# A hybrid decoder step on one core: the second token of each cached compression pair moves to ScalarE's queue, and GpSimd makes one page's product of the sample rows' stick-breaking scores

## The chip, the core and the metric

The kernel runs on one core of one Trainium2 chip, as one program. The metric is the device time of one execution, in microseconds (us). Each time is a median of several executions. The engines are TensorE (PE; its weight loads are PEld), VectorE (DVE), ScalarE (ACT), GpSimd (POOL) and SyncE (SP), which only issues transfers and handles registers. A name with a q (SPq, ACTq) is an engine's instruction queue. Every engine runs its own queue in order, and semaphores order the engines against each other.

## The reference, cut to what matters

The program is one inference step of a one-layer decoder, for a prompt of 512 tokens and for 8 sample rows (one new token each, with 256 cached tokens in two pages of 128). Both go through an input projection, two groups of attention heads, an output projection and a hierarchical mixture of experts. Two pieces of it matter here.

The compression branch folds the cached keys and values, 16 tokens at a time, into blocks (block 32, stride 16):

```python
def compress_blocks(k, pe, w1, w2):
    chunks = k[:, :(nc + ratio - 1) * CMP_STRIDE].reshape(B, nc + ratio - 1, CMP_STRIDE, NSA_KV_HEADS, HEAD_DIM)
    blocks = jnp.concatenate([chunks[:, r:r + nc] for r in range(ratio)], axis=2)
    ...
    hid = jax.nn.gelu(jnp.einsum('bnge,eh->bngh', flat, w1))
    return jnp.einsum('bngh,hd->bngd', hid, w2)
```

The stick-breaking heads of a sample row need, for each of 8 heads, the scores of its query against 256 cached keys of 64 elements:

```python
z = jnp.einsum('bqhd,blhd->bhql', q, k).astype(jnp.float32) / math.sqrt(HEAD_DIM)
```

## The kernel before, in words

**The plan.** Before any instruction is written, the kernel builds one list, `PLAN`, of steps (`step(kind, key)`). Every engine walks this list and emits its own part of each step, so the list is the order of work of all five queues. `Signals` turns the marks made on the way into semaphore values. `side` and `put(slot, ...)` hang further steps on the slots of the projection: slot 2n + half is half `half` of projection tile n. There are 30 tiles, six groups of weight columns (in the order KV4, KV2, SBQ, NQ, SBK, SBV) times five row tiles (four of the prompt with 128 rows, one of the 8 sample rows).

**A projection tile.** TensorE multiplies in two halves of four products (line 2825; 2829 for the 8 rows) into a ring of four PSUM banks. ScalarE copies the result out (2722, 2725). For the groups with rotary positions, GpSimd makes the sine products (2649) and, for some groups, copies (2651 to 2654), counted on the semaphore `swapped`; VectorE makes the cosine product (2785), waits for `swapped` and adds (2787). Two tiles later the tile's results are stored by ScalarE's queue (2592 to 2595) and turned by TensorE (2807). All transposes (`tstep`) go through a ring of two PSUM banks, whose copies alternate between ScalarE (2682) and VectorE (2766, 2768). A transpose waits for the copy of the one two before it.

**The compression pairs.** `pair_step(q)` stands in slots 4 to 25. It turns pair q, 128 rows of two tokens each (`XT`, line 2807 on TensorE), and then plans `load_pair(q + 6)`, as there are PAIRS = 6 buffers. There are 20 pairs: 16 of the cache (eight sample rows, keys and then values) and 4 of the prompt. In `sync_more`, kind "pair" (lines 1033 to 1053), SyncE waits until TensorE has turned pair q - 6 and issues the loads. A cached pair takes four, two pages by two tokens, as every token of a pair lands in its own half of the buffer; a prompt pair takes two (1047). The page numbers come from the input `page_table`: `load_small` (984 to 991) loads it and reads its 16 numbers into registers of SyncE. The same queue carries the compression weights (996) and the next projection weights (2617), interleaved slot by slot. Pairs 0 to 5 are planned ahead of the projection.

**The sample rows' scores.** `query_rows(b)`, for b from 0 to 7, stands in slots 35 to 39, between the last tiles of the group NQ. Its order against the rotation of those tiles is: rotation of NQ tile 2, rounds 0 to 3, rotation of NQ tile 3, rounds 4 to 6, rotation of NQ tile 4, round 7. The query row of b has been stored to memory and is loaded by SyncE spread over all 128 partitions (1064) into one of two buffers; row b + 2 is loaded once round b has been scored (`sb_scored`). Page loads for later steps (1081, 1085, 1088) follow in the same queue. On VectorE a round is, for each of the two pages, a product of 128 x 512 elements (1329) and a sum over the 64 elements of a head (1334).

```python
            for pg in range(NPG):
                n = lq["sbk", 2 * b + pg]
                sg.wait(dve, f"slot{n % SLOTS}", n)
                ins = V.tensor_tensor(product_sb[:, pg, :]...
            link(ins)
```

**What comes behind.** The cached pages of the other branches, the prompt's attention, the output projection, the router and then 16 experts, whose weights (three of 2 MB each) SyncE loads into a ring of eight buffers, each as soon as TensorE is done with it.

Of the kernel before, what the change touches and what calls it, by code (L numbers as in the profile page):

```python
# [15 lines left out]
ALU = mybir.AluOpType  # L16
# [7 lines left out]
P = 128  # L24
D = 1024
SEQ = 512
NB = 8
# [140 lines left out]
def body(nc, ctx, a, out, cf_at, cf_n, cb_at, cb_n):  # L168
# [157 lines left out]
    def query_rows(b):  # L326
        step("qb", b)
        sg.mark("sb_scored", b)
        load_query(b + 2)
        for pg in range(NPG):  # L330
            load_page(lq["sbk", 2 * b + pg] + SLOTS)
# [161 lines left out]
    for n, (cc, i) in enumerate(proj):  # L493
        use("m", ("proj", n), "act")
        norm(n + 2)
        for half in range(2):
            step("proj", n, half)
            if n == 0 and not half:
                transpose_h(1)
            if half:  # L500
                transpose_h(n + 2)
            if half and i == TILES - 1 and n // TILES + 2 < NCH:
                for piece in range(4):
                    put(2 * n + 1 + piece, load_w_more, n // TILES + 2, piece)
            if half and cc >= NQ:
                step("rope", n)
                sg.mark("swapped", n)
# [512 lines left out]
    def pool_page(name, j):  # L1020
        return a[name][0, bass.ds(page_reg[j], 1)].rearrange("o t h d -> (o t) (h d)")

    def sync_more(sp, kind, key):
        if kind == "load_small":
# [7 lines left out]
        elif kind == "pair":  # L1032
            q, = key
            kv, t = order[q]
            if q >= PAIRS:
                sg.wait(sp, "t_full", ("XT", q - PAIRS))
            dst = pair[:, q % PAIRS, :].rearrange("p (g l d) -> p l g d", g=GROUPS, l=2)
            name = "cmp_" + "kv"[kv]
            if t < 2:
                if (kv, t) == (0, 0):  # L1040
                    for i in range(QT):
                        n = pn[KV4, i]
                        sg.wait(sp, f"st_raw{rq[n] % 4}", n)
                        sg.wait(sp, f"st_rot{ri[n] % 2}", n)
                src = out[name + "_p"][0, 0, t * 2 * P:(t + 1) * 2 * P].rearrange("(p l) g d -> p l g d", l=2)
                for l in range(2):
                    sp.dma_start(dst[:, l], src[:, l]).then_inc(sg[f"pair{q % PAIRS}"], 16)
            else:
                for pg in range(NPG):
                    src = a["cache_" + name][0, bass.ds(page_reg[2 * (t - 2) + pg], 1)].rearrange(  # L1050
                        "o (p l) g d -> (o p) l g d", l=2)
                    for l in range(2):
                        sp.dma_start(dst[64 * pg:64 * pg + 64, l], src[:, l]).then_inc(sg[f"pair{q % PAIRS}"], 16)
        elif kind == "q_store":
# [65 lines left out]
    def gps_begin(pool):  # L1120
        nc.gpsimd.iota(token[:, :], [[P, TILES]], base=0, channel_multiplier=1,
                       allow_small_or_imprecise_dtypes=True).then_inc(sg["iota"], 1)

    def gps_more(pool, kind, key):
        if kind == "slots":
            i, = key
# [12 lines left out]
    def act_more(act, link, inverse_rms, kind, key):  # L1139
        if kind == "hid":  # L1140
            kv, = key
# [12 lines left out]
        elif kind == "gates":  # L1154

            sg.wait(act, "swapped", pn[KV2, QT])
            nc.scalar.activation(gates[:, 0:QT, :], gates[:, 0:QT, :], ACT.Exp, scale=-1.0)
# [141 lines left out]
    def dve_more(dve, link, kind, key):  # L1299
# [18 lines left out]
        elif kind == "qb":  # L1318
# [5 lines left out]
            else:  # L1324
                sg.wait(dve, "sb_scored", b - 1)
            for pg in range(NPG):
                n = lq["sbk", 2 * b + pg]
                sg.wait(dve, f"slot{n % SLOTS}", n)
                ins = V.tensor_tensor(product_sb[:, pg, :].rearrange("p (h d) -> p h d", h=HEADS),
                                      page[:, n % SLOTS].rearrange("p s t -> p (s t)").rearrange("p (h d) -> p h d", h=HEADS),  # L1330
                                      q, ALU.mult)
            link(ins)
            for pg in range(NPG):
                ins = V.tensor_reduce(zt[:, 64 * pg + 8 * b:64 * pg + 8 * b + 8],
                                      product_sb[:, pg, :].rearrange("p (h d) -> p h d", h=HEADS), AX.X, ALU.add)
            ins.then_inc(sg["sb_scored"], 1)
        elif kind == "gates":
# [1295 lines left out]
    def _(pool):  # L2633
        gps_begin(pool)
        for kind, key in PLAN:
            if kind == "rope":
# [18 lines left out]
                ins.then_inc(sg["swapped"], 1)  # L2655
            else:
# [76 lines left out]
    def _(dve):  # L2733
# [9 lines left out]
        for kind, key in PLAN:  # L2743
# [26 lines left out]
            elif kind == "rope":  # L2770
# [14 lines left out]
                link(nc.vector.tensor_tensor(dst, src, cos, ALU.mult))  # L2785
                sg.wait(dve, "swapped", n)
                nc.vector.tensor_tensor(dst, dst, sw, ALU.add).then_inc(sg["rotated"], 1)
# [78 lines left out]
```

## Time and profile before

| | before |
|---|---|
| median of 3 runs | 825.58 us (823.18 to 826.46) |
| profiled execution, its own time | 818.89 us |
| its span | 817.1 us |
| TensorE busy | 739.3 us (90%) |
| VectorE / ScalarE / GpSimd busy | 383.6 / 219.6 / 56.4 us |
| mean granted TensorE clock | 0.951 |
| read from and written to memory | 153.08 MB and 21.41 MB |

The profile is of one execution. Its span runs from the first to the last instruction of the program, and its own time lies 1.8 us above that. "Busy" leaves out the issuing of transfers and register work, so a queue that does only these shows no busy time though it is occupied. The granted clock is the share of 2.4 GHz that TensorE was given: 1.00 or, at 1.2 GHz, 0.50.

### The profile page before, as it was taken

The page shows a single profiled execution, that of the slowest core. Times are in us where ns is not written, and L with a number is a line of the kernel's source. Part 1 is how long each engine was busy: PE and PEld are TensorE (multiplying, and loading weights), DVE is VectorE, ACT ScalarE, POOL GpSimd, SP SyncE. Part 2 cuts the span into 40 slices and gives each one's busy share as a digit, 9 for nine tenths or more (in the row PEclk, how much of TensorE's full clock was granted, in tenths as well). Part 3 has the DMA queues.
Part 4 walks back from the last instruction along what each step waited for, and adds up shares of the span by engine and source line. Part 5 has one row for each costly group of instructions (what it writes and reads, how often), then busy time and mean ns, then how long its engine had stood idle before and what let it go on. Part 6 is the DMA issues. An engine that isn't in the chain of part 4 may idle for free.

```text
span 817.1 us, 12103 instructions
## 1 busy us (share of the span) xinstructions
PE 739.3 (90%) x4522; PEld 394.8 (48%) x4522; DVE 383.6 (47%) x884; ACT 219.6 (27%) x561; POOL 56.4 (7%) x87
## 2 busy tenths in 40 slices
PE   4985999979999789989979977789999999999987
PEld 2454456434645544545545543345445456544532
DVE  5421103385220667786876855375323434222236
ACT  1211111111220446656757831001101111010113
POOL 0111000120000000000000000210000000000040
PEclk9999799999999678999989998699999999999999
DMA  8135881548433970000000246698899999999983
GB/s 328 33 94 165 238 315 34 199 129 246 141 128 108 280 286 1 1 3 1 1 27 1 100 161 230 219 322 312 321 397 406 399 382 403 407 400 401 413 323 126
DMA packets 99245, 173.21 MB, mean 212 GB/s; under 512 B 21234, under 2 KB 38354, under 8 KB 99154
## 3 DMA queue, kind: packets, MB, share of 16 engines
q1 hardware_dynamic: 87986, 150.76, 52.0%
q10 hardware_dynamic: 7904, 11.37, 3.7%
q0 software_dynamic: 3296, 10.30, 3.6%
q8 instruction: 37, 0.61, 0.3%
q14 instruction: 22, 0.18, 0.1%
HBM read 153.08 MB, written 21.41 MB: 214 GB/s over the span
## 4 chain that ended last, share of the span: by engine, by line
PE 53%; DVE 8%; DMA 7%; issue 5%; ACT 4%; ACTq 0%; POOL 0%; DVEq 0%; SPq 0%
PE bank L2392 15%; PE bank L2825 6%; PE bank L2383 5%; PE bank L1797 5%; PE bank L2807 4%; PE bank L1724 3%; PE bank L1743 3%; DMA reg<-w_up 3%; PE bank L2426 3%; PE bank L2511 1%; PE bank L2516 1%; DMA work<-h_rows,ids 1%; PE bank L1726 1%; ACT work L2682 1%; PE bank L1635 1%
## 5 line engine op out<-in xcount | busy, mean ns | idle before, releaser
L2825 PE MATMUL bank<-reg 128*128 128x512 f32 (+1 forms) x384 | 167.0, 582 | 1.2 <-DVE reg L2766 0.9
L2392 PE MATMUL bank<-reg,qreg 128*32 128x128 f32 (+2 forms) x880 | 118.1, 373 | 1.0 <-issue 0.8
L2825 PEld LDWEIGHTS bank<-reg 128*128 128x128 f32 x384 | 72.2, 197 | 70.3 <-issue 67.5
L2807 PE MATMUL bank<-cf,reg 128*128 128x128 f32 (+1 forms) x384 | 64.3, 288 | 27.5 <-DVE reg L2757 9.6
L2392 PEld LDWEIGHTS bank<-reg,qreg 128*32 128x32 f32 (+2 forms) x880 | 62.2, 135 | 53.4 <-issue 41.8
L2807 PEld LDWEIGHTS bank<-cf,reg 128*128 128x128 f32 (+1 forms) x384 | 43.8, 147 | 45.8 <-issue 34.6
L1797 PE MATMUL bank<-reg 128*128 128x512 f32 x128 | 64.7, 629 | 0.4 <-DVE x L1504 0.3
L2682 ACT ACTIVATE work<-bank 128x128 f32<-128x128 f32 (+6 forms) x107 | 41.1, 414 | 43.1 <-PE bank L2807 42.5
L2766 DVE COPY work<-bank 128x128 f32<-128x128 f32 (+4 forms) x56 | 23.3, 430 | 54.7 <-PE bank L2807 54.6
L1212 ACT ACTIVATE reg<-bank,st 128x128 f32<-128x128 f32 (+3 forms) x64 | 33.2, 526 | 35.8 <-DVE st L1372 35.7
L2383 PE MATMUL bank<-reg,work 128*128 128x512 f32 x96 | 42.5, 596 | 0.0
L1743 PE MATMUL bank<-work,vreg 128*64 128x128 f32 x480 | 39.4, 296 | 2.7 <-DVE work L2766 2.7
L2180 DVE TENSOR_SCALAR work<-work 128x512 f32<-128x512 f32 (+3 forms) x16 | 5.6, 352 | 72.6 <-ACT work L2088 72.5
L2181 DVE RECIPROCAL work<-work 128x512 f32<-128x512 f32 (+3 forms) x16 | 39.2, 2453 | 0.5
L1743 PEld LDWEIGHTS bank<-work,vreg 128*64 128x64 f32 x480 | 26.8, 143 | 25.0 <-issue 19.5
L1372 DVE TENSOR_REDUCE st<-bank 128x1 f32<-128x128 f32 (+3 forms) x64 | 28.4, 485 | 11.3 <-PE bank L1726 10.9
L1132 POOL DMA_INDIRECT slot_tokens<-token,slots x10 | 9.9, 986 | 320.6 <-DVE slots L1565 318.7
L2101 ACT COPY work<-bank 128x512 f32<-128x512 f32 (+1 forms) x16 | 9.0, 560 | 84.4 <-PE bank L2383 48.5
L1797 PEld LDWEIGHTS bank<-reg 128*128 128x128 f32 x128 | 22.6, 198 | 17.2 <-issue 16.2
L1724 PE MATMUL bank<-vreg,qreg 64*128 64x128 f32 (+3 forms) x128 | 28.6, 523 | 1.4 <-issue 1.0
L2082 ACT COPY qreg<-bank 128x512 f32<-128x512 f32 (+3 forms) x16 | 7.5, 466 | 83.2 <-PE bank L2439 44.3
L2274 DVE COPY work<-bank 128x512 f32<-128x512 f32 (+1 forms) x9 | 5.7, 633 | 51.3 <-PE bank L2383 41.6
(336 smaller groups left out, 940.8 us busy)
## 6 DMA issues: line engine op xcount, KB each, us to landing
reg<-w_gate SPq DMA_DIRECT2D x12, 2048.0 KB, 19.6
reg<-w_up SPq DMA_DIRECT2D x12, 2048.0 KB, 18.7
reg<-w_down SPq DMA_DIRECT2D x12, 2048.0 KB, 20.2
reg<-w_in SPq DMA_DIRECT2D x16, 512.0 KB, 5.8
expert_rows<-vreg SPq DMA_DIRECT2D x11, 512.0 KB, 5.1
reg<-cache_sb_k SPq DMA_DIRECT2D x16, 256.0 KB, 4.5
reg<-cache_sb_v SPq DMA_DIRECT2D x16, 256.0 KB, 4.3
qreg<-w_up SPq DMA_DIRECT2D x2, 2048.0 KB, 14.6
```

Source lines behind the costliest of these rows:

```text
L1212: nc.scalar.activation(prob_of(key, e)[:, 0:n], at(ring, key)[:, 0:n], ACT.Exp, bias=st[:, top:top + 1], accum_out=st[:, col:col + 1]).the ...
L1372: V.tensor_reduce(st[:, top:top + 1], at(ring, key)[:, 0:n], AX.X, ALU.max, negate=True).then_inc(sg["arg"], 1)
L1724: T.matmul(outs[e][:, 0:n], pairs[e][0], pairs[e][1], start=True, stop=False)
L1743: ins = T.matmul(to[64 * e:64 * e + 64, :], v, probT[:, turn_at[key] % 3, e, k * P:(k + 1) * P], start=(k == 0 and b != WIN), stop=(k == i ...
L1797: ins = T.matmul(at(ring, ("wout", i, group))[0:r, :], chunks_of(i)[:, chunk, 0:r], w_out[:, chunk, 512 * half:512 * half + 512], start=(k ...
L2181: link_loop(V.reciprocal(s_, s_), 3 * j + 2)
L2383: ins = T.matmul(out_bank[:, :], lhs[k], rhs[k], start=(k == 0), stop=(k == n - 1))
L2392: ins = T.matmul(bank[which][rows, at_:at_ + w], rowsT[b][:, k, r0:r0 + n], w_[:, k, h * w:(h + 1) * w], start=(k == 0), stop=(k == KD - 1))
L2426: ins = T.matmul(to[rows, 0:w], actsT[j % 2][:, 4 * r0 // P + k % per, q:q + n], w_[:, k, w * h:w * h + w], start=(k == 0), stop=(k == 3))
L2682: ins = nc.scalar.activation(dst, src, ACT.Copy, scale=scale)
L2807: ins = nc.tensor.transpose(dst, src, ident[0:src.shape[0], 0:src.shape[0]])
L2825: ins = nc.tensor.matmul(at("m", ("proj", n))[:, 0:w], hT[:, k, i * P:(i + 1) * P], win[:, pos % 2, k, 0:w], start=(k == 0), stop=(k == KD ...
```

## The change

Three things are changed.

1. For pairs 6 and up, SyncE loads token 0 of each pair of rows and ScalarE's queue loads token 1. ScalarE's part stands in its `act_more`, kind "pair", so in ScalarE's queue right behind its part of the transpose of pair q - 6. At its first such pair, ScalarE waits for the page table and reads the 16 page numbers into registers of its own. Pairs 0 to 5 stay with SyncE.
2. In `query_rows` GpSimd makes the product of page 0 of each round, VectorE that of page 1 and both sums. GpSimd's products alternate between two buffers, and VectorE has a third. VectorE sums its own page first, then waits for GpSimd's.
3. The semaphore `swapped` becomes `pool_part` and counts GpSimd's rotations and its products alike.

```diff
@@ query_rows
         step("qb", b)
+        sg.mark("pool_part", ("qb", b))
         sg.mark("sb_scored", b)
@@ buffers
-    product_sb = view(work, 3584, [2, 512])
+    product_sb = [work[:, 3584:4096], work[:, 4608:5120], work[:, 4096:4608]]
@@ new, used by sync_more and act_more
+    def load_pair_rows(eng, pages_at, tokens, q):
+        kv, t = order[q]
+        if q >= PAIRS:
+            sg.wait(eng, "t_full", ("XT", q - PAIRS))
...
+            for l in tokens:
+                eng.dma_start(dst[:, l], src[:, l]).then_inc(sg[f"pair{q % PAIRS}"], 16)
+            return
+        for pg in range(NPG):
+            src = a["cache_" + name][0, bass.ds(pages_at[2 * (t - 2) + pg], 1)].rearrange("o (p l) g d -> (o p) l g d", l=2)
+            for l in tokens:
+                eng.dma_start(dst[64 * pg:64 * pg + 64, l], src[:, l]).then_inc(sg[f"pair{q % PAIRS}"], 16)
@@ sync_more
...
-                    for l in range(2):
-                        sp.dma_start(dst[64 * pg:64 * pg + 64, l], src[:, l]).then_inc(sg[f"pair{q % PAIRS}"], 16)
+            load_pair_rows(sp, page_reg, (0, 1) if key[0] < PAIRS else (0,), *key)
@@ gps_more
+        if kind == "qb":
+            b, = key
+            n = lq["sbk", 2 * b]
+            sg.wait(pool, f"query{b % 2}", b)
+            sg.wait(pool, f"slot{n % SLOTS}", n)
+            if b >= 2:
+                sg.wait(pool, "sb_scored", b - 2)
+            else:
+                sg.wait(pool, "m_full", ("comp", 1))
+            nc.gpsimd.tensor_tensor(product_sb[b % 2].rearrange("p (h d) -> p h d", h=HEADS), page_rows(n),
+                                    query[:, b % 2, :].rearrange("p (h d) -> p h d", h=HEADS), ALU.mult
+                                    ).then_inc(sg["pool_part"], 1)
@@ act_more
+        if kind == "pair":
+            q, = key
+            if q < PAIRS:
+                return
+            if not act_page_reg:
+                act.wait_ge(sg["pages"], 16)
+                for j in range(NB * NPG):
+                    act_page_reg.append(act.value_load(pages[0:1, j:j + 1], min_val=0, max_val=19))
+            load_pair_rows(act, act_page_reg, (1,), q)
@@ dve_more, kind "qb"
-            for pg in range(NPG):
...
-            ins.then_inc(sg["sb_scored"], 1)
+            n = lq["sbk", 2 * b + 1]
+            sg.wait(dve, f"slot{n % SLOTS}", n)
+            own = product_sb[2].rearrange("p (h d) -> p h d", h=HEADS)
+            link(V.tensor_tensor(own, page_rows(n), q, ALU.mult))
+            V.tensor_reduce(zt[:, 64 + 8 * b:64 + 8 * b + 8], own, AX.X, ALU.add)
+            sg.wait(dve, "pool_part", ("qb", b))
+            V.tensor_reduce(zt[:, 8 * b:8 * b + 8], product_sb[b % 2].rearrange("p (h d) -> p h d", h=HEADS), AX.X, ALU.add
+                            ).then_inc(sg["sb_scored"], 1)
```

## Rows read from the trace of the kernel before

**Rows 1.** The page: the span

```profile
span 817.1 us, 12103 instructions
```

**Rows 2.** Waits of TensorE, 39 to 88 us: engine, line, waited for; us, times, longest

```profile
PE bank L2807 <- DMA work<-cache_cmp_v: 10.4, 8, 2.4
...
PE bank L2807 <- DMA work<-cache_cmp_k: 1.1, 1, 1.1
```

**Rows 3.** Line L1053, pair loads on SyncE's queue: ns min/median/max, starts; time to landing

```profile
L1053 SPq DMA_DIRECT2D work<-cache_cmp_v x32: 598/598/1947, 56.0 to 83.6; - x32
...
DMA to landing us min/median/max: 2.0/2.3/3.9
```

**Rows 4.** Timeline of SyncE's queue, 29 to 55 us: start, duration, merged count

```profile
29.49 25.74 SPq L1053 DMA_DIRECT2D work<-cache_cmp_k  x32
```

**Rows 5.** Line L991, the sixteen register reads on SyncE's queue

```profile
L991 SPq TENSOR_LOAD <-pages x16: 260/264/473, 20.3 to 28.8; - x16
```

**Rows 6.** Line L1948, the one register read on ScalarE's queue

```profile
L1948 ACTq TENSOR_LOAD <-extra_i x1: 480/480/480, 790.7 to 790.7; - x1
...
L1948 ACTq SEQ_ASSERT  x1: 29/29/29, 791.4 to 791.4; - x1
```

**Rows 7.** Timeline, 35 to 40 us: ScalarE, its queue, TensorE

```profile
35.14 0.39 ACTq L2592 DMA_DIRECT2D out_cmp_k_p<-reg  x1
...
36.72 0.45 ACTq L2592 DMA_DIRECT2D out_sel_v_p<-reg  x1
...
38.62 0.59 ACT L2722 COPY reg<-bank 128x512 f32<-128x512 f32 x1 [3.10 <-PE bank L2825]
...
39.45 0.41 PE L2807 MATMUL bank<-cf,work 128*128 128x128 f32 x2 [0.28 <-ACT reg L2682]
```

**Rows 8.** Timeline, 64 to 92 us: TensorE's pair transposes, its first full projection

```profile
64.82 0.44 PE L2807 MATMUL bank<-cf,work 128*128 128x128 f32 x2 [1.94 <-DMA work<-cache_cmp_v]
...
67.77 0.44 PE L2807 MATMUL bank<-cf,work 128*128 128x128 f32 x2 [0.62 <-DMA work<-cache_cmp_v]
...
70.44 0.44 PE L2807 MATMUL bank<-cf,work 128*128 128x128 f32 x2 [0.24 <-DMA work<-cache_cmp_v]
...
86.85 5.55 PE L2825 MATMUL bank<-reg 128*128 128x512 f32 x7
```

**Rows 9.** Stretches: busy PE, PEld, DVE, ACT, POOL; PEclk, DMA share, GB/s

```profile
80.00:86.80 6.80, 3.18 (x39) 1.92 (x39) 1.06 (x4) 1.09 (x6) 0.63 (x2) 0.59 0.75 213
86.80:91.50 4.70, 4.70 (x7) 2.08 (x8) 0.36 (x2) 0.39 (x2) 0.44 (x3) 0.50 0.81 199
182.00:187.00 5.00, 5.00 (x9) 2.60 (x10) 4.29 (x7) 0.60 (x1) 0.00 (x0) 0.50 0.78 232
560.00:700.00 140.00, 140.00 (x1060) 74.62 (x1060) 49.22 (x87) 17.21 (x37) 8.24 (x9) 1.00 1.01 381
```

**Rows 10.** Timeline, 170 to 193 us: SyncE's queue, VectorE, TensorE

```profile
170.32 0.34 SPq L1064 DMA_DIRECT2D work<-query_rows  x1
...
174.68 1.93 DVE L1329 TENSOR_TENSOR work<-reg,work 128x512 f32<-128x512 f32 x2 [1.74 <-DMA work<-query_rows]
...
182.00 1.12 PE L2807 MATMUL bank<-cf,reg 128*128 128x128 f32 x4 [5.37 <-DVE reg L2787]
...
188.08 1.30 DVE L1329 TENSOR_TENSOR work<-reg,work 128x512 f32<-128x512 f32 x2 [0.28 <-DMA work<-query_rows]
...
192.64 0.41 PE L2807 MATMUL bank<-cf,reg 8*128 8x8 f32 x4 [0.64 <-DVE reg L2787]
```

**Rows 11.** Line L1334, VectorE's sums; line L1064, the query rows' loads

```profile
L1334 DVE TENSOR_REDUCE work<-work x16: 675/681/687, 169.0 to 194.4; 128x8 f32<-128x512 f32 x16
...
DMA to landing us min/median/max: 3.3/4.1/5.0
```

**Rows 12.** Timeline, 163 to 166 us: GpSimd's two rotary products of one tile

```profile
163.83 1.23 POOL L2649 TENSOR_TENSOR reg<-reg,cf 128x256 f32<-128x256 f32 x1 [6.67 <-ACT reg L2722]
165.02 0.72 POOL L2649 TENSOR_TENSOR reg<-reg,cf 128x256 f32<-128x256 f32 x1
```

More of the change, by code:

```diff
@@ L506, in body @@
                 step("rope", n)
-                sg.mark("swapped", n)
+                sg.mark("pool_part", n)
                 sg.mark("rotated", n)
@@ L1021, in pool_page @@
         return a[name][0, bass.ds(page_reg[j], 1)].rearrange("o t h d -> (o t) (h d)")
+    def load_pair_rows(eng, pages_at, tokens, q):
+        kv, t = order[q]
+        if q >= PAIRS:
+            sg.wait(eng, "t_full", ("XT", q - PAIRS))
+        dst = pair[:, q % PAIRS, :].rearrange("p (g l d) -> p l g d", g=GROUPS, l=2)
+        name = "cmp_" + "kv"[kv]
+        if t < 2:
+            if (kv, t) == (0, 0):
+                for i in range(QT):
+                    n = pn[KV4, i]
+                    sg.wait(eng, f"st_raw{rq[n] % 4}", n)
+                    sg.wait(eng, f"st_rot{ri[n] % 2}", n)
+            src = out[name + "_p"][0, 0, t * 2 * P:(t + 1) * 2 * P].rearrange("(p l) g d -> p l g d", l=2)
+            for l in tokens:
[5 more added lines that the diff above has]
+                eng.dma_start(dst[64 * pg:64 * pg + 64, l], src[:, l]).then_inc(sg[f"pair{q % PAIRS}"], 16)
+    act_page_reg = []
     def sync_more(sp, kind, key):
@@ L1032, in sync_more @@
         elif kind == "pair":
[L1033 to L1045, printed above, removed]
-                for l in range(2):
-                    sp.dma_start(dst[:, l], src[:, l]).then_inc(sg[f"pair{q % PAIRS}"], 16)
-            else:
-                for pg in range(NPG):
-                    src = a["cache_" + name][0, bass.ds(page_reg[2 * (t - 2) + pg], 1)].rearrange(
-                        "o (p l) g d -> (o p) l g d", l=2)
-                    for l in range(2):
-                        sp.dma_start(dst[64 * pg:64 * pg + 64, l], src[:, l]).then_inc(sg[f"pair{q % PAIRS}"], 16)
+            load_pair_rows(sp, page_reg, (0, 1) if key[0] < PAIRS else (0,), *key)
         elif kind == "q_store":
@@ L1122, in gps_begin, with page_rows @@
                        allow_small_or_imprecise_dtypes=True).then_inc(sg["iota"], 1)
+    def page_rows(n):
+        return page[:, n % SLOTS].rearrange("p s t -> p (s t)").rearrange("p (h d) -> p h d", h=HEADS)
     def gps_more(pool, kind, key):
-        if kind == "slots":
+        if kind == "qb":
[10 more added lines that the diff above has]
+                                    ).then_inc(sg["pool_part"], 1)
+        elif kind == "slots":
             i, = key
@@ L1139, in act_more @@
     def act_more(act, link, inverse_rms, kind, key):
-        if kind == "hid":
+        if kind == "pair":
[7 more added lines that the diff above has]
+            load_pair_rows(act, act_page_reg, (1,), q)
+        elif kind == "hid":
             kv, = key
@@ L1154, in act_more @@
         elif kind == "gates":
-            sg.wait(act, "swapped", pn[KV2, QT])
+            sg.wait(act, "pool_part", pn[KV2, QT])
             nc.scalar.activation(gates[:, 0:QT, :], gates[:, 0:QT, :], ACT.Exp, scale=-1.0)
@@ L1325, in dve_more @@
                 sg.wait(dve, "sb_scored", b - 1)
[L1326 to L1335, printed above, removed]
-            ins.then_inc(sg["sb_scored"], 1)
+            n = lq["sbk", 2 * b + 1]
[6 more added lines that the diff above has]
+                            ).then_inc(sg["sb_scored"], 1)
         elif kind == "gates":
@@ L2654, in _ @@
                     ins = nc.gpsimd.tensor_copy(gates[0:r, i, :], raw[0:r, rq[n] % 4, 256:280])
-                ins.then_inc(sg["swapped"], 1)
+                ins.then_inc(sg["pool_part"], 1)
             else:
@@ L2785, in _ @@
                 link(nc.vector.tensor_tensor(dst, src, cos, ALU.mult))
-                sg.wait(dve, "swapped", n)
+                sg.wait(dve, "pool_part", n)
                 nc.vector.tensor_tensor(dst, dst, sw, ALU.add).then_inc(sg["rotated"], 1)
```

## The prediction

> **What bounds the kernel now.** I began with the page [rows 1]: the span is 817.1 us, the profiled execution's own time 818.89, and the runs' median 825.58, 6.69 above it. I work in differences and add them to the median. Next came the two stages that the change touches, and then whether a saving there survives to the end.
>
> The first stage runs from 35 to 92 us. TensorE does the first projections, and in nearly every half tile it also turns one pair of cached compression rows. Its waits name the loads of those rows [rows 2]: 10.4 + 1.1 = 11.5 us. SyncE's queue explains them. It issues four loads a pair at 0.60 us each [rows 3], the first 32 at 25.74 / 32 = 0.80 us a load with the register work between [rows 4]. A pair so takes about 3 us of queue, and each half tile adds a weight load. From 64.82 to 70.44 TensorE makes a tile with two pairs in 5.62 us, of which 0.62 and 0.24 are waits: the work is 4.76 us, 2.4 a pair [rows 8]. So SyncE's issuing is the bound. The idle time also costs clock: the granted clock is 0.59 from 80 to 86.8 us and 0.50 (1.2 GHz) to 91.5 us [rows 9].
>
> The second stage runs from 168 to 195 us: eight rounds of the sample rows' scores on VectorE. TensorE wants the transposes of a rotated query tile and waits 5.37 us, to 182.00, then 0.64 us more, to 192.64 [rows 10]: that tile's rotation stands on VectorE behind four rounds. Some rounds wait themselves for the query row's load, which lands 3.3 to 5.0 us after issue [rows 11].
>
> Late in the kernel TensorE is busy 140.00 of 140 us while the DMA engines are full too [rows 9]. But its weight loads are issued when TensorE has freed their buffers, so work that comes earlier brings its loads earlier, and I carry a saving to the end one to one.
>
> **What the change gives, part one: the pairs.** For pairs 6 to 15 SyncE issues two loads instead of four, for the four prompt pairs one instead of two. That is 20 x 0.8 = 16 us of queue less. What stays a pair is 2 x 0.75 us and 0.6 for a weight load, 2.1, under TensorE's 2.4. Each load is wanted six half tiles after its buffer is free, some 14 us, against 2.3 to land [rows 3]. So I take all waits of [rows 2] away: -11.5 us. The low clock that followed goes with them: TensorE was busy 3.18 and 4.70 us in the two stretches at about half speed [rows 9], half of which comes back: -3.9. Together -15.4 us.
>
> **What it costs.** At its first pair ScalarE reads the page numbers into registers, sixteen of them. SyncE's sixteen start between 20.3 and 28.8 us [rows 5], 8.5 / 15 = 0.57 us each, 9.1 in all. ScalarE's one read of this kind takes 0.48 with a wait attached, its range check starts 0.7 us after it [rows 6], so 0.75 to 0.78 with the check. I take 0.57: SyncE's first read, also with a wait, is the 0.473 of [rows 5] and the rest fall to 0.264. The upper end is 16 x 0.78 = 12.5; the lower is the read, the register step and the check without gaps, 0.43 x 16 = 6.9.
>
> These reads sit in ScalarE's queue, in order, and this is where they hurt. They begin where the first store of a compression tile stands now, 35.14 [rows 7], right after the first pair's copy. 35.14 + 9.1 = 44.2; two loads at 0.75 make 45.7; the four stores behind them take about 0.5 each, 2.0, so 47.7; then the projection's copy and the transposed tile's copy, from 38.62 to 39.45 now, 0.8: 48.6. TensorE's second pair transposes wait for that last copy through the two transpose banks; now they start at 39.45 [rows 7]. So TensorE stands still for 48.6 - 39.45 = 9.2 us. Nothing covers it: in plan order all that TensorE has next needs that bank. Half clock follows: after the 5.37 us standstill the clock stayed at 0.50 for 5.0 busy us, 182 to 187 [rows 9]. The same again costs 2.5 us.
>
> Afterwards ScalarE issues two loads a pair, near 1.5 us, beside stores of 0.5 each. For a tile of two pairs: 2.9 of pair loads, 1.0 to 1.9 of stores, 0.2 of dispatch, 4.1 to 5.0 us against TensorE's 4.76 [rows 8]. Three tiles are a little over, one bank of slack is there, and I take 1.0 us of new waits; 0 if the issues hide. Part one: -15.4 + 9.2 + 2.5 + 1.0 = **-2.7 us**.
>
> **Part two: the scores.** VectorE's round is two products and two sums, 2 x 0.65 + 2 x 0.68 = 2.66 us (1.30 for a pair of products at 188.08 [rows 10], 0.68 a sum [rows 11]). One product goes to GpSimd. Its price stands in no row: a rotary product of 256 columns takes 0.72 us [rows 12], so 512 take at most 1.44; I take 1.4. When both engines multiply, one is held: the same form took 1.23 beside a product of VectorE [rows 12], 0.5 more, and VectorE's two took 1.93 instead of 1.30 at 174.68 beside GpSimd [rows 10]. A round that begins when its query lands is then 1.4 + 0.5 on GpSimd and 0.68 for the last sum: 2.6 us, nothing gained. Only a round whose query is there already (1 and 3 in front of the rotation) saves a product, 0.65 each. GpSimd's own part of the rotation now stands behind product 3, two operations of 0.72, 1.44 us; it is done about when VectorE has finished round 3, so it costs nothing, and up to 1.4 if not. VectorE's new wait, for GpSimd's product before the last sum, has the next round, the rotation and a transpose's copy behind it; GpSimd's waits (query, page, the sum of two rounds ago) have only the rotation. At 182.00 this gives -1.3 us. The rounds after it hang on query loads issued two rounds before (170.32 to 174.68, for one [rows 10]), on SyncE. At 192.64 I keep **-0.7 us**; the bounds are +2 and -2.
>
> A rule of the Trainium skill speaks against this part: its page "SBUF — State Buffer", in the section on the single rule, says that a VectorE instruction with two inputs in SBUF and a GpSimd instruction that reads SBUF exclude each other for a whole instruction. By that rule VectorE's product would wait for all of GpSimd's 1.4 us whenever GpSimd starts first. The trace shows a hold of 0.5 us of 0.72, so it agrees with the kind and not clearly with the size.
>
> **The sum.** -2.7 - 0.7 = -3.4 us: 818.89 becomes 815.5 on the profiled execution, and the median 825.58 becomes 822.2. A measurement of this kernel can tell about 0.5% from no change, 4.1 us, so that is "the same", narrowly.
>
> **The rivals.** *ScalarE's standstill is cheap.* If the reads run without gaps (6.9 us instead of 9.1, -2.2) and its issues hide (-1.0), the sum is -6.6: 819.0. For it: nothing in [rows 6] forbids it, as ScalarE shows one read alone. Against it: SyncE's sixteen have the gaps.
>
> *ScalarE's queue is the new bound.* Reads at 0.78 add 12.5 - 9.1 = 3.4 us; an issue of 1.1 instead of 0.75 us adds 1.4 a tile, over three tiles 4.2. Sum -3.4 + 3.4 + 4.2 = +4.2, 829.8. It decides once a ScalarE issue costs more than (4.76 - 1.2) / 4 = 0.9 us. For it: the only read on that engine; against it: its stores go at 0.39 to 0.45 [rows 7].
>
> *The lock costs VectorE.* If VectorE's product always waits for all of GpSimd's, a round with a fresh query is 1.4 + 0.65 + 2 x 0.68 = 3.4, 0.75 longer. Three such rounds in the chain of queries turn -0.7 into +1.6: sum -1.1, 824.5, no change.
>
> *The change does less than it says.* It leaves pairs 0 to 5 wholly to SyncE, whose first 24 loads take to 49 us [rows 4]; pairs 6 to 8 could still be late, +1 at most, as TensorE itself is late by then.
>
> **Chances.** The forecast 0.35, with 0.05 of it spilling over -4.1; the lock 0.10; the cheap standstill 0.35; ScalarE as the bound 0.20. So faster 0.40, same 0.40, slower 0.20. The range takes in the cheap end with a little of part two (816) and the slow end (830).
>
> **What would show it.** In the changed profile: sixteen reads on ScalarE's queue near 35 us at 0.57; TensorE idle from 39.2 to about 48.6, released by ScalarE's copy; half clock for about 5 us behind it; no waits on the second cache's loads, and full clock at 87 us. In the scores: GpSimd's product at 1.4, 1.9 beside VectorE's; the transposes of 182.00 about 4 us earlier in all, 2.7 of them from the pairs. I am wrong if TensorE doesn't stand still at 39, if its waits for pairs stay, or if the difference between the kernels changes much behind 200 us.

## The result: slower, and the profile after

| | before, same chip | after |
|---|---|---|
| median of 4 runs | 824.38 us (815.65 to 826.46) | 832.11 us (828.88 to 833.96) |
| ratio after / before | | 1.0125, 95% interval 1.0071 to 1.0179 |
| profiled execution, its own time (span) | 818.89 us (817.1) | 832.79 us (830.9) |
| mean granted TensorE clock | 0.951 | 0.935 |

The change costs 7.7 us by the medians and some 10 us by the ratio. The forecast was 822.2, in a range of 816 to 830.

The page of the profile after, with the span, the engines' busy time and the DMA queue that carries the issues of ScalarE. That queue had 7904 packets and 11.37 MB before, GpSimd was busy 56.4 us:

```profile
span 830.9 us, 12177 instructions
...
PE 747.9 (90%) x4522; PEld 400.2 (48%) x4522; DVE 381.6 (46%) x876; ACT 219.1 (26%) x561; POOL 68.8 (8%) x95
...
q10 hardware_dynamic: 11872, 12.29, 4.2%
```

Both traces have 4522 TensorE matmul records in the same order. So the start of the n-th record in after, minus its start in before, is a running account of the change:

| start in before, us | start in after | difference |
|---|---|---|
| 39.45 | 49.51 | +10.1 |
| 41.96 | 54.14 | +12.2 |
| 60.57 | 76.66 | +16.1 |
| 74.88 | 86.89 | +12.0 |
| 91.28 | 95.77 | +4.5 |
| 120.27 | 124.67 | +4.4 |
| 182.00 | 188.22 | +6.2 |
| 192.64 | 198.51 | +5.9 |
| 206.59 | 213.82 | +7.2 |
| 538.41 | 548.76 | +10.4 |
| 811.16 (last) | 824.95 | +13.8 |

So the first stage leaves +4.5 us where -2.7 was forecast. From there to 206.59 another 2.7 are added, where the second stage should have given 0.7 back; but only 1.5 of them stand at its end, at 192.64 (+4.4 to +5.9). The other 1.3 come in a stretch of half clock behind it, shown below. One such difference is of two single executions: five kernels below leave the first stage as it is in before, and at 91.28 they stand between -1.4 and -0.1. What comes later belongs to neither stage and is taken up at the end.

**The first stage.** TensorE's waits in after, from 39 to 120 us, and behind them those from 120 to 215 (engine, line, waited for; us, times, longest). L2834 is now the line of all transposes:

```profile
PE bank L2834 <- ACT reg L2709: 10.1, 1, 10.1
PE bank L2834 <- DVE work L2793: 7.0, 4, 3.8
...
PE bank L2834 <- DVE reg L2814: 7.2, 1, 7.2
```

The waits for the cached rows [rows 2] are gone. One wait of 10.1 us for ScalarE stands in their place, and four for a copy of VectorE, 7.0 us (in before there are two of these, 2.0 us).

Line L1168 of after, the sixteen reads on ScalarE's queue (ns min/median/max; first and last start):

```profile
L1168 ACTq TENSOR_LOAD <-pages x16: 271/274/475, 35.3 to 43.8; - x16
L1168 ACTq FUSED_REGOPS  x16: 147/147/173, 35.8 to 44.1; - x16
L1168 ACTq SEQ_ASSERT  x16: 18/18/29, 36.0 to 44.3; - x16
```

They start where the first store stood [rows 7], and (43.8 - 35.3) / 15 = 0.57 us is the price of one, as on SyncE [rows 5]. The timeline after them, 44 to 50 us, shows what was queued behind: two pair loads, four stores, the projection's copy, the transposed tile's copy, and then TensorE:

```profile
44.54 1.95 ACTq L1044 DMA_DIRECT2D work<-cache_cmp_k  x2
46.59 0.55 ACTq L2619 DMA_DIRECT2D out_cmp_k_p<-reg  x1
...
48.19 0.45 ACTq L2619 DMA_DIRECT2D out_sel_v_p<-reg  x1
48.68 0.58 ACT L2749 COPY reg<-bank 128x512 f32<-128x512 f32 x1 [12.95 <-issue]
49.16 0.20 ACT L2709 ACTIVATE reg<-bank 128x32 f32<-128x32 f32 x1
...
49.51 0.66 PE L2834 MATMUL bank<-cf,work 128*128 128x128 f32 x2 [10.14 <-ACT reg L2709]
```

From 68 to 77 us the same queue is late in another way: pair loads, the third store 2.6 us after the first of them, VectorE's rotation waiting 6.72 us for that store to land (it writes into the stored buffer), VectorE's copy behind the rotation, and TensorE waiting 3.77 us for the copy:

```profile
68.41 1.40 ACTq L1044 DMA_DIRECT2D work<-cache_cmp_v  x2
...
71.02 0.48 ACTq L2619 DMA_DIRECT2D out_sel_k_p<-reg  x1
...
75.49 0.29 DVE L2812 TENSOR_TENSOR reg<-reg,cf 128x128 f32<-128x128 f32 x1 [6.72 <-DMA out_sel_k_p<-reg]
...
76.03 0.48 DVE L2793 COPY work<-bank 128x128 f32<-128x128 f32 x2
...
76.66 0.20 PE L2834 MATMUL bank<-cf,reg 8*128 8x8 f32 x1 [3.77 <-DVE work L2793]
```

The trace of after has several stretches in which the granted clock was half, 1.2 GHz; these are five of them. The first three lie in the first stage, the fourth behind the second, and the last far behind the change (columns as in [rows 9]):

```profile
43.80:54.00 10.20, 4.49 (x7) 2.17 (x8) 0.92 (x2) 1.13 (x4) 1.30 (x3) 0.50 0.33 80
64.30:67.70 3.40, 3.40 (x10) 2.49 (x9) 0.52 (x2) 1.48 (x6) 1.33 (x3) 0.50 0.44 116
77.90:81.30 3.40, 3.40 (x10) 2.50 (x9) 0.40 (x1) 0.84 (x3) 1.00 (x4) 0.51 0.43 125
...
211.10:214.50 3.40, 3.40 (x7) 1.51 (x5) 2.12 (x4) 1.35 (x4) 0.00 (x0) 0.50 0.72 246
549.00:555.80 6.80, 5.97 (x13) 3.02 (x12) 4.67 (x18) 0.58 (x1) 0.96 (x1) 0.50 1.02 390
```

The first begins in the standstill, the next two 1.5 and 1.2 us behind a wait of TensorE (1.86 us to 62.79, 3.77 us to 76.66). The stretch of before from 80 to 91.5 us [rows 9] is gone. Before has none like the fourth (its clock is 1.00 from 204 to 210 us); e2 and e4, which have the pairs part and not the scores part, have one like it, from 208.2 and from 210.8 us. The line of e2:

```profile
208.20:211.60 3.40, 3.40 (x8) 1.85 (x8) 2.07 (x4) 1.59 (x5) 0.00 (x0) 0.50 0.73 281
```

So the 1.3 us that are added there can't be put down to the scores.

**The second stage.** Timeline of after, 169 to 189 us: GpSimd, VectorE, TensorE:

```profile
170.10 2.94 POOL L1143 TENSOR_TENSOR work<-reg,work 128x512 f32<-128x512 f32 x2
170.23 1.67 DVE L2814 TENSOR_TENSOR reg<-reg 128x512 f32<-128x512 f32 x1 [1.37 <-POOL reg L2676]
171.83 1.27 DVE L1367 TENSOR_SCALAR gates<-gates 128x96 f32<-128x96 f32 x1
...
184.47 1.93 POOL L2676 TENSOR_TENSOR reg<-reg,cf 128x256 f32<-128x256 f32 x2
...
186.36 1.26 POOL L1143 TENSOR_TENSOR work<-reg,work 128x512 f32<-128x512 f32 x1
186.50 1.66 DVE L2814 TENSOR_TENSOR reg<-reg 128x512 f32<-128x512 f32 x1 [0.68 <-POOL reg L2676]
...
188.22 1.11 PE L2834 MATMUL bank<-cf,reg 128*128 128x128 f32 x4 [7.19 <-DVE reg L2814]
```

GpSimd's product takes 1.26 us alone. VectorE's rotation add (L2814), 0.69 us when alone, takes 1.66 and 1.67 when it starts 0.14 us after such a product. The product has 1.12 us left by then; the add is 0.97 longer and ends 0.54 us after the product (186.36 + 1.26 = 187.62 against 188.16). The query tile's transposes start at 188.22 after a wait of 7.19 us, which was 5.37 [rows 10].

### The profile page after: what moved, and what is told of

It reads as the page before. It is cut to its first block, busy times and chain, and to the rows that moved or that the text cites. A ratio compares the mean times of both kernels' runs of the same rounds, so it can differ in the third digit from the quotient of the medians.

```text
span 830.9 us, 12177 instructions
## 1 busy us (share of the span) xinstructions
PE 747.9 (90%) x4522; PEld 400.2 (48%) x4522; DVE 381.6 (46%) x876; ACT 219.1 (26%) x561; POOL 68.8 (8%) x95
## 4 chain that ended last, share of the span: by engine, by line
PE 54%; DVE 7%; DMA 7%; issue 5%; ACT 4%; POOL 1%; ACTq 0%; DVEq 0%; POOLq 0%
PE bank L2419 15%; PE bank L2852 7%; PE bank L2410 5%; PE bank L1824 5%; PE bank L2834 4%; PE bank L1751 3%; DMA reg<-w_up 3%; PE bank L1770 3%; PE bank L2453 3%; DMA work<-h_rows,ids 1%; ACT work L2709 1%; PE bank L2538 1%; PE bank L2543 1%; PE bank L2402 1%; PE bank L1753 1%
## 5 line engine op out<-in xcount | busy, mean ns | idle before, releaser
L2852 PE MATMUL bank<-reg 128*128 128x512 f32 (+1 forms) x384 | 171.9, 596 | 1.2 <-DVE reg L2793 0.9
L2852 PEld LDWEIGHTS bank<-reg 128*128 128x128 f32 x384 | 74.9, 204 | 72.3 <-issue 68.8
L2834 PE MATMUL bank<-cf,reg 128*128 128x128 f32 (+1 forms) x384 | 64.8, 290 | 33.6 <-DVE reg L2784 9.6
L2834 PEld LDWEIGHTS bank<-cf,reg 128*128 128x128 f32 (+1 forms) x384 | 44.3, 148 | 52.3 <-issue 34.8
L1399 DVE TENSOR_REDUCE st<-bank 128x1 f32<-128x128 f32 (+3 forms) x64 | 28.3, 483 | 12.8 <-PE bank L1753 12.5
L2749 ACT COPY reg<-bank 128x512 f32<-128x512 f32 (+1 forms) x20 | 10.9, 546 | 77.3 <-PE bank L2852 64.3
L1824 PEld LDWEIGHTS bank<-reg 128*128 128x128 f32 x128 | 22.7, 198 | 17.5 <-issue 16.5
L2068 POOL DMA_INDIRECT work<-h_rows,ids x15 | 13.9, 929 | 203.4 <-PE bank L2466 100.2
L2301 DVE COPY work<-bank 128x512 f32<-128x512 f32 (+1 forms) x9 | 5.7, 632 | 53.5 <-PE bank L2410 43.8
## 6 DMA issues: line engine op xcount, KB each, us to landing
qreg<-w_up SPq DMA_DIRECT2D x2, 2048.0 KB, 14.6
```

The costliest lines, as they stand in the source:

```text
L1399: V.tensor_reduce(st[:, top:top + 1], at(ring, key)[:, 0:n], AX.X, ALU.max, negate=True).then_inc(sg["arg"], 1)
L1824: ins = T.matmul(at(ring, ("wout", i, group))[0:r, :], chunks_of(i)[:, chunk, 0:r], w_out[:, chunk, 512 * half:512 * half + 512], start=(k ...
L2834: ins = nc.tensor.transpose(dst, src, ident[0:src.shape[0], 0:src.shape[0]])
L2852: ins = nc.tensor.matmul(at("m", ("proj", n))[:, 0:w], hT[:, k, i * P:(i + 1) * P], win[:, pos % 2, k, 0:w], start=(k == 0), stop=(k == KD ...
```

## The experiments

Every kernel was timed in five rounds against the kernel before, on the same chip. The theories at the start: the pairs lose by ScalarE's reads (a standstill of TensorE) and by late stores; the scores lose by the lock between VectorE and GpSimd. The rivals: the order of the queries alone decides the second stage; the loads on ScalarE are slow in themselves.

**e1_reads_only.** The kernel before, and ScalarE reads the sixteen page numbers at its first such pair, unused.

```diff
@@ act_more, before
+        if kind == "pair":
+            if key[0] == PAIRS:
+                act.wait_ge(sg["pages"], 16)
+                for j in range(NB * NPG):
+                    act.value_load(pages[0:1, j:j + 1], min_val=0, max_val=19)
```

> The kernel before, with one addition: at ScalarE's place behind pair 0's copy it reads the sixteen page numbers into registers that nothing uses. Standstill theory: TensorE idles from 39.2 to about 46.5 to 47 us (reads 9.1 us, the four stores 2.0 behind them, no pair loads of ScalarE), 7.5 us, and the clock falls after it; but the pair loads of SyncE go on meanwhile, so part of the 11.5 us of waits for pairs is hidden behind it: the kernel is 2 to 6 us slower than before. Rival, ScalarE has slack there and the reads are covered: the same as before within 1 us, with no idle time at 39 us. Rival, the slower time comes from the engines behind 215 us: the same as before up to 90 us and no change in the median.

Measured: 820.90 us against 820.82, ratio 0.9997 (0.9960 to 1.0034). TensorE's waits in it, 36 to 95 us:

```profile
PE bank L2812 <- ACT reg L2687: 8.4, 1, 8.4
PE bank L2812 <- DMA work<-cache_cmp_v: 3.2, 2, 1.8
PE bank L2812 <- DVE work L2771: 2.5, 4, 1.5
```

The standstill is there in full, and it costs nothing, where 2 to 6 us had been expected: waits for the rows fall from 11.5 to 3.2 us, and the running difference goes from +8.7 at 39.45 to +6.0 at 64.82, +2.3 at 74.88 and +0.4 at 82.28. SyncE's queue bounded this stage and ran on while TensorE stood. A standstill of one engine is free as long as another sets the pace.

**e2_pairs_only.** The kernel after with VectorE's two products as before (change 2 taken back).

```diff
@@ dve_more, after
-            link(V.tensor_tensor(own, page_rows(n), q, ALU.mult))
...
+            for pg in range(NPG):
+                n = lq["sbk", 2 * b + pg]
...
@@ gps_more, after
-            nc.gpsimd.tensor_tensor(product_sb[b % 2]...
```

> The changed kernel with its scores part undone (both products on VectorE as before); pairs shared between SyncE and ScalarE. If the traces' running difference holds (4.5 us later at 91 us), it is 3.5 to 5.5 us slower than before, with 10 us of idle time of TensorE at 39 to 49 us and 5 us of waits for VectorE's copies in the compression tiles. Rival, pairs are a gain as forecast and the scores are the loss: 2 to 4 us faster than before.

Measured: 826.97 us, ratio 1.0080 (1.0048 to 1.0113), so 6.2 us by the medians. Its waits in the first stage are those of after (10.6 for ScalarE, 6.8 for VectorE). The difference is +3.0 us at 120, +3.2 at 192.64 and +4.8 at 206, behind its stretch of half clock. The pairs alone are slower.

**e3_scores_only.** The kernel after with both tokens on SyncE's queue again.

```diff
@@ sync_more, after
-            load_pair_rows(sp, page_reg, (0, 1) if key[0] < PAIRS else (0,), *key)
+            load_pair_rows(sp, page_reg, (0, 1), *key)
@@ act_more, after
...
-            load_pair_rows(act, act_page_reg, (1,), q)
+            return
```

> The changed kernel with its pairs part undone (all loads on SyncE); GpSimd makes one product a round. If the running difference holds (4.5 us at 91 us, 7.2 at 215), it is 2 to 3 us slower than before, TensorE's wait near 182 us is 7 instead of 5.4 us, and VectorE's rotation add takes 1.66 us beside GpSimd's product of 1.26. Rival, the lock is of no weight, as forecast: 0.5 to 1.5 us faster.

Measured: 822.61 us, ratio 1.0031 (0.9999 to 1.0063), 1.8 us by the medians and 2.5 by the ratio. The interval holds 1, as do those of e6 and e11 below, which also have this part without the pairs and also come out a little slower (1.0020, 1.0026). So a loss is not shown by the times. In e3's trace TensorE's wait near 182 us is 5.7 us, where 7 was expected, and the difference goes from -0.8 at 120 to -0.3 at 192.64: the stage costs 0.5 us. What is as expected is the rotation add. Timeline of e3, 164 to 168 us:

```profile
164.88 2.94 POOL L1143 TENSOR_TENSOR work<-reg,work 128x512 f32<-128x512 f32 x2
165.02 1.67 DVE L2807 TENSOR_TENSOR reg<-reg 128x512 f32<-128x512 f32 x1 [1.37 <-POOL reg L2669]
166.61 1.27 DVE L1360 TENSOR_SCALAR gates<-gates 128x96 f32<-128x96 f32 x1
```

**e4_early_reads.** Pairs as in after, scores as before, and ScalarE's reads moved to four places around the norms of row tiles 3 and 4, ahead of the projection.

```diff
@@ act, kind "norm", against e2
...
+                read_pages(act, {3: 4, 4: 14}.get(i, 0))
                 inverse_rms(small[0:ROWS[i], i:i + 1], D, "rstd", ("attn", i))
+                read_pages(act, {3: 10, 4: 16}.get(i, 0))
```

> Pairs shared as in the changed kernel, scores as before, but ScalarE reads its page numbers in four lots around the norms of tiles 3 and 4, where it idles (24 to 35 us). Standstill theory: no idle time of 10 us at 39 us, so about 10 us less than the kernel with the pairs part alone, plus up to 2.5 us of half clock: 4 to 9 us faster than before. What stays is 0 to 5 us of waits for VectorE's copies, whose rotation waits for stores that stand behind pair loads in ScalarE's queue. Rival, ScalarE's issues are the new bound whatever the reads do: the same as before within 2 us.

Measured: 817.96 us, ratio 0.9956 (0.9926 to 0.9985), 2.9 us faster than before and 9.0 faster than e2 on the same chip. The wait of 10.6 us for ScalarE is 0.9. So the place of the reads is worth 9 us here, and it was worth nothing in e1: the difference between the two is whether the loads are shared. VectorE's copies are waited for as in e2 (7.4 us), and VectorE's rotations wait 12.5 us, three times, for the third store (`out_sel_k_p`) to land, and 11.0 for two others. The difference is -7.3 us at 91 and -0.0 at the end: most of it goes in three places, +1.7 us between 206 and 250, where a stretch of half clock begins at 210.8, +1.3 from 250 to 300, and +2.6 between 538 and 542.

**e5_stores_first.** e4, with ScalarE's pair loads held back until the tile's stores are issued.

```diff
@@ act, the walk through PLAN, against e4
             elif kind == "store":
                 store(act, *key)
+                for k in held:
+                    act_more(act, link, inverse_rms, "pair", k)
+                held.clear()
+            elif kind == "pair":
+                held.append(key)
```

> The kernel of e4_early_reads, with ScalarE's pair loads held back until the stores of the projection tile stand in its queue. Theory: what is left of the loss in the pairs part is VectorE's rotation, waiting for the stores of the tile before last (12.5 us of its idle time) and so late with its copies, for which TensorE waits 7.4 us between 36 and 95 us. With the stores ahead these waits fall to 2 to 4 us and the kernel is 2 to 5 us faster than e4_early_reads, 5 to 8 us faster than before. Rival, ScalarE's queue is full whatever the order: within 1.5 us of e4_early_reads.

Measured: 812.04 us against 821.05, ratio 0.9891 (0.9844 to 0.9938). Faster, but not by the expected way. VectorE's waits for that store are gone (12.5 to none; 8.8 for the two others stay), and TensorE's waits on VectorE only fell from 7.4 to 6.2. Waits of e5, 36 to 95 us, and its timeline, 50 to 54 us:

```profile
PE bank L2835 <- DVE work L2794: 6.2, 4, 1.8
PE bank L2835 <- ACT work L2703: 1.7, 1, 1.7
PE bank L2835 <- ACT reg L2703: 1.6, 1, 1.6
```

```profile
50.45 0.58 ACT L2750 COPY reg<-bank 128x512 f32<-128x512 f32 x1 [1.71 <-PE bank L2853]
51.07 0.43 DVE L2813 TENSOR_TENSOR reg<-reg,cf 128x256 f32<-128x256 f32 x1 [3.67 <-ACT reg L2750]
51.12 1.10 POOL L2669 TENSOR_TENSOR reg<-reg,cf 128x128 f32<-128x128 f32 x2 [8.83 <-ACT reg L2750]
52.56 0.42 DVE L2815 TENSOR_TENSOR reg<-reg 128x256 f32<-128x256 f32 x1 [1.06 <-POOL vreg L2671]
52.90 0.48 DVE L2794 COPY work<-bank 128x128 f32<-128x128 f32 x2
53.53 0.30 PE L2835 MATMUL bank<-cf,reg 128*128 128x128 f32 x1 [1.54 <-DVE work L2794]
```

This is what is late next once the loads are on time: ScalarE's copy, the rotation on GpSimd and VectorE, and only then VectorE's copy of the pair that TensorE needs. Three of the four waits are of this kind, 4.5 us; the fourth, 1.6, still stands behind a store (`out_win_k_p`, for which a rotation waits 3.9). In the traces e5 is no earlier than e4 at 91 us (-5.2 against -7.3). e4's trace has a stretch of half clock at 535.1 us, of 6.8 us, and e5's has none. So why e5's median is lower than e4's is not settled by these runs, and the two were timed on different chips.

**e6_four_queries.** e3 with four buffers for the query rows instead of two.

```diff
-    query = view(work, 5120, [2, 512])
+    query = view(work, 5120, [4, 512])
...
-        load_query(b + 2)
+        load_query(b + 4)
```

> The kernel of e3_scores_only with four buffers for query rows instead of two, so that no round waits for a query load; the order of rounds and rotations is as before. Theory: a round that waits for its query gains nothing from GpSimd; without these waits rounds follow each other at about 2.1 us, TensorE's wait near 182 us falls from 5.4 to 3 to 4 us (its rotation still stands behind four rounds and behind GpSimd's products), and it is 1 to 4 us faster than e3_scores_only. Rival, the lock between VectorE and GpSimd is the whole loss: no faster than e3_scores_only.

Measured: 822.41 us, ratio 1.0020 (0.9984 to 1.0055). TensorE's wait in the second stage falls to 3.4 us, and in the trace the stage gives 2.2 us (-1.4 at 120, -3.6 at 206), yet the median does not fall. Of the traced execution's gain 1.9 us go between 790 and 800, in a stretch of half clock that begins at 792.3. In the stage VectorE's product meets GpSimd's rotation and its next product, one right behind the other, and is held through both, 2.85 us:

```profile
182.36 1.39 POOL L2674 TENSOR_TENSOR reg<-reg,cf 8x256 f32<-8x256 f32 x2
182.68 2.85 DVE L1357 TENSOR_TENSOR work<-reg,work 128x512 f32<-128x512 f32 x1
183.72 1.25 POOL L1148 TENSOR_TENSOR work<-reg,work 128x512 f32<-128x512 f32 x1
```

**e7_rounds_behind.** The kernel before with four query buffers and the rounds in later slots, so that rotations stand ahead of them on VectorE.

```diff
...
-        put((35, 35, 36, 36, 37, 38, 38, 39)[b], query_rows, b)
+        put((35, 35, 37, 37, 39, 39, 40, 41)[b], query_rows, b)
```

> The kernel before (both products on VectorE, pairs by SyncE) with four query buffers and the rounds planned in slots 35, 35, 37, 37, 39, 39, 40, 41, so each rotation stands ahead of the rounds beside it. Theory: the 5.4 and 0.6 us waits of TensorE at 182 and 192 us go, and with them 2.5 us of half clock; VectorE ends its last round near 192 us, for which TensorE may wait 2 to 4 us further back: 3 to 7 us faster than before. Rival, the waits only move to the next transposes: the same as before.

Measured: 820.07 us, ratio 0.9991 (0.9960 to 1.0022). The waits of 182 and 192 us are gone and the difference is -8.8 us at 192.73, but one new wait stands behind it, and it is -2.2 at 199. Waits of e7, 160 to 215 us:

```profile
PE bank L2812 <- DVE work L1339: 4.7, 1, 4.7
```

L1339 is the last sum of the last round, for the transpose of all scores. The wait had moved, as the rival said.

**e8_both_moved.** e7's order and GpSimd's product together (e6 with that order).

> The kernel of e7_rounds_behind with GpSimd's product as in the change. Theory: with the queries there and the rotations ahead, a round is about 2.1 us on VectorE instead of 2.7 and GpSimd's product hides: 1 to 3 us faster than e7_rounds_behind. Rival, the lock holds VectorE's products and rotations for GpSimd's 1.26 us each time GpSimd starts first: no faster than e7_rounds_behind, or up to 2 us slower.

Measured: 817.22 us, ratio 0.9958 (0.9922 to 0.9993). The same wait is 3.9 us. With queries and rotations out of the way a round takes 2.1 us on VectorE, 0.56 less than the 2.66 of before. Timeline of e8, 184 to 187 us:

```profile
184.65 0.69 DVE L1357 TENSOR_TENSOR work<-reg,work 128x512 f32<-128x512 f32 x1
184.73 1.74 POOL L1148 TENSOR_TENSOR work<-reg,work 128x512 f32<-128x512 f32 x1 [3.34 <-DVE work L1360]
...
186.75 0.69 DVE L1357 TENSOR_TENSOR work<-reg,work 128x512 f32<-128x512 f32 x1
```

Here VectorE starts first and is not held; GpSimd pays 0.48 us (1.74 for 1.26), beside VectorE's sums. The median is 2.9 us under e7's on the same chip. By the traces the stage gives 3.1 us here (-1.1 at 120, -4.2 at 206), 2.1 in e7 and 2.2 in e6, so about 1 us of it is seen there. Of the four kernels with GpSimd's product and the loads on SyncE (e3, e6, e8, e11) this is the only one whose time falls; that the order of start is what does it is argued, not shown.

**e9_all.** e5's pairs and e8's scores in one kernel.

> Both parts of the change, each mended: page numbers read early, ScalarE's pair loads behind the stores (e5_stores_first), and four query buffers with the rotations ahead of the rounds and GpSimd's product (e8_both_moved). Theory: the two stages are independent, TensorE's running times add: 9 us from the first and 3.4 from the second, 11 to 13 us faster than before. Rival, the second stage takes up what the first gives (its queries and pages then come too late): 8 to 10 us.

Measured: 809.83 us against 820.70, ratio 0.9888 (0.9841 to 0.9935). Against e5's 0.9891 nothing more can be told from the times alone, though the difference in the trace is -10.1 us at 91.28, -15.6 at 182.00 and -14.6 at 196.52, -10.4 at the end.

**e10_later_scores.** e9 with the transpose of all scores one slot later.

```diff
-    put(43, tstep, "zT")
+    put(44, tstep, "zT")
```

> The kernel of e9_all with the transpose of all scores one slot later, where TensorE waited 3.9 us for VectorE's last round in e8_both_moved. Theory: 3.6 us of projection stand between, so the wait goes and it is 1 to 3.5 us faster than e9_all. Rival: the wait only moves to the page transposes, whose copies stand on VectorE behind the last round: within 1 us of e9_all.

Measured: 808.34 us, ratio 0.9879 (0.9828 to 0.9931). The wait of 3.9 us is gone, and 2.6 us on another copy of VectorE and 0.9 us on a page load have come. It isn't told apart from e9. It is the fastest kernel of the study, 12.4 us below before by the medians.

**e11_gpsimd_held.** e3, where GpSimd's first two products wait until VectorE has done the gates.

```diff
@@ gps_more, against e3
-                sg.wait(pool, "m_full", ("comp", 1))
+                sg.wait(pool, "gates", 0)
```

> The kernel of e3_scores_only, but GpSimd's first two products wait until VectorE has made the gates. Theory of the exclusive lock: VectorE's rotation add falls from 1.67 to 0.69 us and its scaling of the gates from 1.27 to 0.2, so its first own product starts 2 us earlier; GpSimd's two products then stand beside the products and sums of rounds 0 and 1, and hold VectorE's own product for up to 1.3 us once: 0 to 2 us faster than e3_scores_only. Rival, those two instructions were long for another reason: they stay at 1.67 and 1.27.

Measured: 821.94 us, ratio 1.0026 (0.9990 to 1.0061). Timeline, 165 to 168 us, the same two instructions as in e3:

```profile
165.69 0.69 DVE L2807 TENSOR_TENSOR reg<-reg 128x512 f32<-128x512 f32 x1 [1.36 <-POOL reg L2669]
166.30 0.20 DVE L1360 TENSOR_SCALAR gates<-gates 128x96 f32<-128x96 f32 x1
```

0.69 instead of 1.67 us and 0.20 instead of 1.27, with nothing changed but when GpSimd multiplies. That shows the lock. It isn't worth anything in the median, and the wait for the query tile is 6.5 us, no less than e3's 5.7: the rounds behind hang on their queries, and the query tile's rotation add, not held in e3 (0.69), starts 0.14 us behind a product here and takes 1.67 us. Which of the two engines starts first differs from kernel to kernel and round to round: in e3 GpSimd is 0.02 us ahead at 184.52, and VectorE's product takes 1.79; in after VectorE is 0.05 ahead at 179.66 and takes 0.69.

## Why the prediction was wrong

**The standstill: right.** Forecast 9.2 us to 48.6, measured 10.1 to 49.51. The reads cost 0.57 each as forecast. Of the 0.9 us more, 0.3 stand before the two pair loads (44.54 for 44.2) and 0.5 in them (1.95 for 1.5).

**"I take all waits of [rows 2] away": right.** No wait for the cached rows is left, and the clock is full at 87 us. (The sum of 20 loads less counts the ten cached pairs alone; with the four prompt pairs it is 24. No later number rests on it.)

**"I take 1.0 us of new waits": this is the first step that failed.** It asked only whether ScalarE's issues fit beside TensorE's 4.76 us a tile, not what waits for their landing and what comes due when the loads no longer do. VectorE's copies cost 7.0 us instead of 2.0, so 5.0. The longest, 3.8, is the store behind the pair loads: VectorE's rotation writes into that store's buffer. The next, 1.9, is the chain of copy, rotation, copy, which had been hidden under the loads: it has no store in it, and e5, with the third store out of the way, keeps 4.5 us of such waits.

**"The same again costs 2.5 us": right for one, but there were three.** The stretch behind the standstill holds 4.49 busy us, half of which is 2.2. But half clock came back three times in the stage, with 4.49 + 3.40 + 3.40 us busy; half of these is 5.6. With the measured terms the account is -11.5 - 3.9 + 10.1 + 5.6 + 5.0 = +5.3 us, where the running difference shows +4.5. My own sum had -2.7: the new waits account for 4.0 of what is missing, the clock for 3.1 and the standstill for 0.9.

**"At 192.64 I keep -0.7 us": the second step that failed.** Measured +1.5 in after (+4.4 at 120 us to +5.9), +0.5 in e3 and +0.3 in e11, against +0.2 in e2, which lacks this part. So the stage gave nothing, and by how much it lost lies within what two traces of one stage differ by. The step at fault is the price of the lock. GpSimd's product takes 1.26, not 1.4. But I let one product be held by 0.5 us, whoever starts first. That is what GpSimd pays when VectorE starts first (1.77 for 1.26). When GpSimd starts first, VectorE stands for nearly all that is left of the longer product (1.67 for 0.69, and 2.85 behind a rotation and a product). Both were in the trace of before, and I misread them. In [rows 12] GpSimd's instruction of 1.23 us stood behind the first of VectorE's two instructions below, over at 164.47; and of the 1.93 us in [rows 10] VectorE's second product, which started behind one of GpSimd's, took 1.21:

```profile
163.78 0.69 DVE L2785 TENSOR_TENSOR reg<-reg,cf 128x512 f32<-128x512 f32 x1 [3.36 <-ACT reg L2722]
...
175.40 1.21 DVE L1329 TENSOR_TENSOR work<-reg,work 128x512 f32<-128x512 f32 x1
```

GpSimd's started at 163.83, so 0.64 us of VectorE's were left, and it was held for 0.51. The right comparison was with these 0.64 us, not with the 0.72 of GpSimd's own instruction. The Trainium skill's page "SBUF — State Buffer", in the section on the single rule, has it so: the two exclude each other for a whole instruction. I had weighed it and gone by the row; the row and the runs agree with the page. What I had as a rival, "the lock costs VectorE", is this, and its +1.6 was near what after shows; it named the products, though, and in after the instruction held on the path is the rotation add. GpSimd's own rotation stood behind product 3 and cost another 0.68 us, which I had bounded at 1.4 and put at nothing. The rounds that hang on queries gained nothing, as forecast.

**The rivals.** "ScalarE's queue is the new bound" came nearest with 829.8, for a wrong reason: its reads took 0.57, and its later issues about 0.7 (1.40 for two at 68.41), under the 0.9 us from which it was to decide. What bound was what stood behind them. "The standstill is cheap" was right for e1 alone. "The change does less than it says" is out: the waits for pairs 6 to 8 were none.

**"I carry a saving to the end one to one": half right.** By 206.59 us the loss is 7.2, near the 7.7 us of the medians; the profiled pair shows 13.8. Of the 6.6 between, 2.4 come between 538 and 542 us of before, where the difference goes from +10.4 to +12.8 into the stretch at 549.0 shown above. In e4 nothing is left of -7.3 at the end, in e9 -10.4 of -13.8. Between the stages and the end of one execution 3 us and more come and go, as much as the whole forecast of -3.4.

## What to carry to other kernels

Before work is moved to another engine's queue, list what is queued behind it there, down to the stores whose landing frees a buffer: the sixteen reads cost 9 us where they stood, and a few steps earlier the wait of 10.6 us that they made was 0.9. A standstill costs only if no other queue sets the pace at that time, so undoing one bound also makes stalls dear that were free. Where GpSimd and VectorE both read two inputs in SBUF, price each overlap by what is left of the other engine's instruction, and keep a rotation or copy that TensorE waits for from starting just behind GpSimd's product.

## What the runs showed of the hardware that I had not expected

- The hold between the two engines is the same both ways: whoever starts second waits for what is left of the other's instruction, less 0.13 to 0.15 us. GpSimd behind VectorE: 0.61 to 0.65 us left, held for 0.48 to 0.51 (1.74 to 1.77 for 1.26). VectorE behind GpSimd: 1.12 left, held for 0.97 (1.66 for 0.69); in e6 2.29 left, held for 2.16 (2.85). The sizes differ only because a product takes 1.26 us on GpSimd and 0.69 on VectorE. An instruction with one input is held too: the gates' scaling took 1.27 instead of 0.20 us. VectorE's sums beside GpSimd kept 0.68.
- Half clock also comes far behind the change, and not at the same places in kernels that do the same work there. A stretch of 6.8 us near 540 us is in the traces of after, e3, e4 and e7, and in none of before, e1, e2, e5, e6, e8, e9, e10 and e11. In after it holds 5.97 busy us, half of them lost, so 3 us. Another, of 3.4 us near 790 us, is in e6, e9 and e11 alone. The seventeen runs of before beside e9 spread from 812.9 to 826.8. Whether such stretches make part of this spread wasn't tested, and what sets them off stays open.
